# Stick-breaking attention with hi and lo parts stacked on 128 rows: two passes for scores and outputs, and suffix sums over pre-added key blocks

## What is computed

```python
h = xn @ w_in                      # [u | q | k | v | gate_a | gate_b]
z = einsum('bqhd,bkhd->bhqk', q, k) * (SB_HEAD_DIM ** -0.5)      # 8 heads of 64
causal = k_pos[None, :] < q_pos[:, None]
log_not = where(causal, log_sigmoid(-z), 0.0)
suffix = cumsum(log_not, axis=3, reverse=True) - log_not
a = where(causal, exp(log_sigmoid(z) + suffix), 0.0)
o = einsum('bhqk,bkhd->bqhd', a, v)
merged = gate_a * (y_pool @ w_pool_up) + gate_b * (o @ w_sb_up)
x = x + merged @ w_out             # then MLP, per-layer embedding, final norm
```

## Time and profile before

| | us |
|---|---|
| median of 3 runs (range) | 812.07 (811.01 to 812.73) |
| the profiled execution's own time | 810.67 |
| its span, first to last instruction | 808.9 |
| TensorE busy in the span | 790.2 |
| VectorE busy | 472.6 |
| ScalarE busy | 372.5 |
| GpSimd busy | 98.7 |

### The profile page before, as it was taken

The page is one execution under the profiler, slowest core; times in us unless marked ns, Lnnn a source line. Parts: engine busy times, 40 slices in busy tenths (PEclk is TensorE's granted clock), DMA queues, the critical chain, the costliest instruction groups (busy, mean ns, idle before and its releaser), DMA issues.

```text
span 808.9 us, 14398 instructions
## 1 busy us (share of the span) xinstructions
PE 790.2 (98%) x6130; PEld 778.7 (96%) x6130; DVE 472.6 (58%) x553; ACT 372.5 (46%) x426; POOL 98.7 (12%) x167
## 2 busy tenths in 40 slices
PE   8999999999999999999999999999999999999994
PEld 8999999999999989999999999999999999999993
DVE  6664444354356536687774257533773367677976
ACT  7444434433485343465652146422552146556543
POOL 1040140051060000010001100010001100100001
PEclk9999999999999999999999999999999999999998
DMA  6333131121221303967564865667574865825502
GB/s 231 119 119 106 66 110 61 66 92 54 91 76 44 106 27 120 294 167 176 168 201 131 196 190 178 171 172 183 167 200 121 204 193 168 211 70 141 147 1 111
DMA packets 32954, 110.19 MB, mean 136 GB/s; under 512 B 4480, under 2 KB 4480, under 8 KB 32896
## 3 DMA queue, kind: packets, MB, share of 16 engines
q1 hardware_dynamic: 24624, 84.72, 31.8%
q0 software_dynamic: 6016, 21.04, 14.5%
q10 hardware_dynamic: 2256, 3.60, 1.3%
HBM read 94.33 MB, written 4.52 MB: 122 GB/s over the span
## 4 chain that ended last, share of the span: by engine, by line
PE 90%; DVE 5%; ACT 2%; issue 1%; DMA 1%; SPq 0%; DVEq 0%
PE psum L1278 23%; PE psum L1023 19%; PE psum L1029 19%; PE psum L1026 19%; PE psum L1076 3%; PE psum L1004 2%; PE psum L1006 2%; PE psum L1005 2%; DMA raw<-w_tiles 1%; DVE work L1398 1%; DVE w_lo L1374 1%; PE psum L1356 1%; DVE xt L1818 0%; DVE b_lo L1730 0%; DVE a_lo L1594 0%
## 5 line engine op out<-in xcount | busy, mean ns | idle before, releaser
L670 ACT ACTIVATE w_hi<-raw_more 128x1024 fp32r<-128x1024 f32 x84 | 88.7, 1056 | 134.9 <-PE psum L1029 102.3
L1023 PE MATMUL psum<-b_hi,w_hi 128*128 128x272 f32 x688 | 142.3, 288 | 0.0
L1029 PE MATMUL psum<-b_hi,w_lo 128*128 128x272 f32 x688 | 142.1, 288 | 0.0
L1026 PE MATMUL psum<-b_lo,w_hi 128*128 128x272 f32 x688 | 141.9, 288 | 0.0
L1023 PE MATMUL psum<-a_hi,w_hi 128*128 128x272 f32 x576 | 121.4, 292 | 2.2 <-DVE a_lo L1388 1.9
L1382 DVE TENSOR_TENSOR w_lo<-raw_more,w_hi 128x1024 fp32r<-128x1024 f32 x84 | 102.4, 1223 | 35.6 <-ACT w_hi L670 35.4
L1029 PE MATMUL psum<-a_hi,w_lo 128*128 128x272 f32 x576 | 119.1, 288 | 0.0
L1026 PE MATMUL psum<-a_lo,w_hi 128*128 128x272 f32 x576 | 118.8, 288 | 0.0
L1278 PE MATMUL psum<-u_hi,w_hi 128*128 128x272 f32 x560 | 116.0, 288 | 1.0 <-issue 0.9
L1278 PE MATMUL psum<-u_hi,w_lo 128*128 128x272 f32 x560 | 115.7, 288 | 0.0
L1278 PE MATMUL psum<-u_lo,w_hi 128*128 128x272 f32 x560 | 115.5, 287 | 0.0
(11 more groups left out here) (207 smaller groups left out, 1006.4 us busy)
## 6 DMA issues: line engine op xcount, KB each, us to landing
raw_more<-w_tiles SPq DMA_DIRECT2D x84, 512.0 KB, 4.4
raw<-w_tiles SPq DMA_DIRECT2D x67, 512.0 KB, 3.5
raw_more<-w_tiles POOLq DMA_DIRECT2D x16, 512.0 KB, 7.0
raw_more<-raw_more POOLq DMA_DIRECT2D x14, 512.0 KB, 8.1
xt<-x_t SPq DMA_DIRECT2D x8, 272.0 KB, 5.0
y_t<-xt SPq DMA_DIRECT2D x8, 272.0 KB, 2.5
raw<-w_tiles POOLq DMA_DIRECT2D x4, 512.0 KB, 7.2
raw_more<-raw POOLq DMA_DIRECT2D x3, 512.0 KB, 5.6
```

Source lines behind the costliest of these rows:

```text
L670: act.activation(w_hi[:, t % W_RING, :, :].rearrange("p k c -> p (k c)"), src, ACT.Copy)\
L1023: pe.matmul(base[:, h, :], w_hi[:, s, wk, :], at(hi, k, h * HALF, (h + 1) * HALF), start=(opens and q == 0), stop=False, skip_group_check= ...
L1026: pe.matmul(base[:, h, :], w_hi[:, s, wk, :], at(lo, k, h * HALF, (h + 1) * HALF), start=False, stop=False, skip_group_check=True)
L1029: mm = pe.matmul(base[:, h, :], w_lo[:, s, wk, :], at(hi, k, h * HALF, (h + 1) * HALF), start=False, stop=(closes and q == len(ks) - 1), s ...
```

## The change

Scores: q's hi part of a head is put on all 128 rows (ScalarE writes its 64 rows, VectorE copies them to the other 64), the keys' hi part on the head's rows and the lo part on the other rows of one block. One pass gives hi by hi and lo by hi together; a second streams q's lo part, with zeros on the other rows (`q_low`, zeroed by GpSimd at the start). Outputs: the stationary block of a head is its v hi columns beside its v lo columns, so that one pass gives two halves of the output rows; p hi and p lo make two passes, and `head_out` copies one half from PSUM and adds the other. Sums: a key block's own and its next block are as before (the next one for one query block alone); what comes from later blocks is first added on VectorE (`stick_later`, three additions of 128 columns), cut in hi and lo (384 columns, ScalarE and VectorE) and added in one pass each. In pairs 0 to 2, `gate(3, i)` moves ahead of `stick_lo`. The new `later` buffers lie in the space of the cached keys and values, whose two loads move from behind pair 0 to behind the last `prob`.

```diff
+        later_hi = nc.alloc_sbuf_tensor_at("later_hi", [P, 3 * P], F32R, offset=place[1])
+        later_lo = nc.alloc_sbuf_tensor_at("later_lo", [P, 3 * P], F32R, offset=place[1] + 3 * P * 4)
         ckt = at(1, "ckt", [P, PAIRS, PAST])
+        later = nc.alloc_sbuf_tensor_at("later", [P, 3 * P], F32, offset=place[1])
...
+        vst = ysb[:, :, SEQ:TOK]
...
+        v_parts = b_hi[:, VOF:VOF + 2 * QB * P].rearrange("p (b n d) -> p b n d", b=QB, d=DH)
+        V_HI, V_LO = slice(0, 4, 3), slice(1, 3)
+        q_low = (b_hi[:, QLO:QLO + SEQ], q_low1[:, :])
...
+            for hh in range(2):
+                pool.memset(q_low[hh].bitcast(F32), 0.0).then_inc(const_made, 1)
...
                 act.activation(b_hi[:, SOF:SOF + Z_COLS], work[:, :], ACT.Copy).then_inc(shi_done, 1)
+                act.wait_ge(later_done, g + 1)
+                act.activation(later_hi[:, :], later[:, :], ACT.Copy).then_inc(laterhi_done, 1)
...
-                act.activation(b_hi[:, QOF:QOF + TOK], ev[:, 0, 0:TOK], ACT.Copy).then_inc(qkhi_done, 1)
+                for hh in range(2):
+                    r = rows_of(hh)
+                    act.activation(b_hi[r, QOF + hh * SEQ:QOF + (hh + 1) * SEQ], ev[r, 0, 0:SEQ], ACT.Copy)\
+                       .then_inc(qkhi_done, 1)
...
-                act.activation(b_hi[:, KOF:KOF + TOK], ev[:, 1, 0:TOK], ACT.Copy).then_inc(qkhi_done, 1)
+                for hh in range(2):
+                    r = rows_of(hh)
+                    act.activation(b_lo[r, KOF + hh * SEQ:KOF + (hh + 1) * SEQ], ev[r, 1, 0:SEQ], ACT.Copy)\
+                       .then_inc(qkhi_done, 1)
...
-            act.dma_start(ckt[:, :, :], ck_t).then_inc(past_in, 16)
-            act.dma_start(cvn[:, :, :], cv).then_inc(past_in, 16)
...
             prob(1, PAIRS - 1)
+            act.dma_start(ckt[:, :, :], ck_t).then_inc(past_in, 16)
+            act.dma_start(cvn[:, :, :], cv).then_inc(past_in, 16)
             prob_hi(1, PAIRS - 1)
...
             def scores(hh, i):
-                r = slice(DH * hh, DH * hh + DH)
-                if hh == 0:
-                    pe.wait_ge(qklo_done, 2 * i + 2)
+                pe.wait_ge(qklo_done, 6 * i + 5 + hh)
                 for b in range(QB):
                     z = z_ps[:, Z_OFF[b]:Z_OFF[b] + Z_LEN[b]]
-                    keys = slice(KOF + P * b, KOF + P * (b + 1))
-                    qs = slice(QOF + P * b, QOF + SEQ)
-                    mm = product(z, b_hi[r, keys], b_lo[r, keys], b_hi[r, qs], b_lo[r, qs], b != 3, b != 1)
+                    keys = slice(KOF + hh * SEQ + P * b, KOF + hh * SEQ + P * (b + 1))
+                    both = slice(QOF + hh * SEQ + P * b, QOF + (hh + 1) * SEQ)
+                    pe.matmul(z, b_lo[:, keys], b_hi[:, both], start=(b != 3), stop=False, skip_group_check=True)
+                    mm = pe.matmul(z, b_lo[:, keys], q_low[hh][:, P * b:SEQ], start=False, stop=(b != 1),
+                                   skip_group_check=True)
                 mm.then_inc(z_done, 1)
...
+                sticks = [(b_hi[:, SOF:SOF + Z_COLS], later_hi), (b_lo[:, SOF:SOF + Z_COLS], later_lo)]
                 for b in range(QB):
-                    for c in range(b, QB):
-                        lhs = negtri if c == b else negone
-                        z = z_ps[:, Z_OFF[b] + P * (c - b):Z_OFF[b] + Z_LEN[b]]
-                        for part in (b_hi, b_lo):
-                            mm = pe.matmul(z, lhs[:, :], part[:, SOF + Z_OFF[c]:SOF + Z_OFF[c] + Z_LEN[c]],
-                                           start=False, stop=(c == QB - 1), skip_group_check=True)
+                    at_b = Z_OFF[b]
+                    for own, _ in sticks:
+                        mm = pe.matmul(z_ps[:, at_b:at_b + Z_LEN[b]], negtri[:, :], own[:, at_b:at_b + Z_LEN[b]],
+                                       start=False, stop=(b == QB - 1), skip_group_check=True)
+                    if b == QB - 1:
+                        continue
+                    nxt = Z_OFF[b + 1]
+                    for own, _ in sticks:
+                        mm = pe.matmul(z_ps[:, at_b + P:at_b + 2 * P], negone[:, :], own[:, nxt:nxt + P],
+                                       start=False, stop=(b == QB - 2), skip_group_check=True)
+                    if b < QB - 2:
+                        more = (slice(0, 2 * P), slice(2 * P, 3 * P))[b]
+                        for _, sums_of in sticks:
+                            mm = pe.matmul(z_ps[:, at_b + 2 * P:at_b + Z_LEN[b]], negone[:, :], sums_of[:, more],
+                                           start=False, stop=True, skip_group_check=True)
                 mm.then_inc(c_done, 1)
...
-                    vs = slice(VOF + P * b, VOF + P * (b + 1))
+                    vs = slice(VOF + P * (2 * b + hh), VOF + P * (2 * b + hh + 1))
                     ps = slice(SOF + Z_OFF[b], SOF + Z_OFF[b] + Z_LEN[b])
-                    mm = product(o_ps[:, P * b:SEQ], b_hi[:, vs], b_lo[:, vs], b_hi[:, ps], b_lo[:, ps],
-                                 b == 0, b == QB - 1)
+                    pe.matmul(o_ps[:, P * b:SEQ], b_hi[:, vs], b_hi[:, ps], start=(b == 0), stop=False,
+                              skip_group_check=True)
+                    mm = pe.matmul(o_ps[:, P * b:SEQ], b_hi[:, vs], b_lo[:, ps], start=False, stop=(b == QB - 1),
+                                   skip_group_check=True)
                 mm.then_inc(o_done, 1)
...
+            def stick_later(hh, i):
+                g = 2 * i + hh
+                one, two, three = (work[:, Z_OFF[b]:Z_OFF[b] + Z_LEN[b]] for b in (1, 2, 3))
+                dve.wait_ge(spm_done, g * QB + QB)
+                dve.tensor_tensor(later[:, 2 * P:3 * P], two[:, P:2 * P], three, ALU.add).then_inc(later_part, 1)
+                dve.tensor_tensor(later[:, 0:P], one[:, P:2 * P], two[:, 0:P], ALU.add)
+                dve.wait_ge(later_part, g + 1)
+                dve.tensor_tensor(later[:, P:2 * P], one[:, 2 * P:3 * P], later[:, 2 * P:3 * P], ALU.add)\
+                   .then_inc(later_done, 1)
             def stick_lo(hh, i):
                 dve.wait_ge(shi_done, 2 * i + hh + 1)
-                dve.tensor_tensor(b_lo[:, SOF:SOF + Z_COLS], work[:, :], b_hi[:, SOF:SOF + Z_COLS],
-                                  ALU.subtract).then_inc(slo_done, 1)
+                dve.tensor_tensor(b_lo[:, SOF:SOF + Z_COLS], work[:, :], b_hi[:, SOF:SOF + Z_COLS], ALU.subtract)
+                dve.wait_ge(laterhi_done, 2 * i + hh + 1)
+                dve.tensor_tensor(later_lo[:, :], later[:, :], later_hi[:, :], ALU.subtract).then_inc(slo_done, 1)
...
             def head_out(hh, i):
-                r = slice(DH * hh, DH * hh + DH)
+                r = rows_of(hh)
                 dve.wait_ge(o_done, 2 * i + hh + 1)
-                dve.tensor_copy(ysb[r, i, 0:SEQ], o_ps[r, :]).then_inc(y_done, 1)
+                dve.tensor_copy(ysb[r, i, 0:SEQ], o_ps[rows_of(1 - hh), :]).then_inc(y_part, 1)
+                dve.wait_ge(y_part, 2 * i + hh + 1)
+                dve.tensor_tensor(ysb[r, i, 0:SEQ], o_ps[r, :], ysb[r, i, 0:SEQ], ALU.add).then_inc(y_done, 1)
...
-                dve.wait_ge(qkhi_done, 2 * i + 1)
-                dve.tensor_tensor(b_lo[:, QOF:QOF + TOK], q, b_hi[:, QOF:QOF + TOK], ALU.subtract)\
-                   .then_inc(qklo_done, 1)
+                for hh in range(2):
+                    r, twice = rows_of(hh), slice(QOF + hh * SEQ, QOF + (hh + 1) * SEQ)
+                    dve.wait_ge(qkhi_done, 4 * i + 1 + hh)
+                    dve.tensor_copy(b_hi[rows_of(1 - hh), twice], b_hi[r, twice]).then_inc(qklo_done, 1)
+                    dve.tensor_tensor(q_low[hh][r, :], q[r, 0:SEQ], b_hi[r, twice], ALU.subtract)\
+                       .then_inc(qklo_done, 1)
                 split(AHEAD + 1, i, S1_PER)
...
-                dve.wait_ge(qkhi_done, 2 * i + 2)
-                dve.tensor_tensor(b_lo[:, KOF:KOF + TOK], k, b_hi[:, KOF:KOF + TOK], ALU.subtract)\
-                   .then_inc(qklo_done, 1)
+                for hh in range(2):
+                    r, keys = rows_of(hh), slice(KOF + hh * SEQ, KOF + (hh + 1) * SEQ)
+                    dve.wait_ge(qkhi_done, 4 * i + 3 + hh)
+                    dve.tensor_tensor(b_lo[rows_of(1 - hh), keys], k[r, 0:SEQ], b_lo[r, keys], ALU.subtract)\
+                       .then_inc(qklo_done, 1)
                 split(AHEAD + 2, i, S1_PER)
...
                     split(AHEAD + 3, i, S1_PER)
+                    stick_later(0, i)
...
+                    stick_later(1, i)
                     split(AHEAD + 7, i, S1_PER)
...
                 else:
+                    gate(3, i)
+                    stick_later(1, i)
                     stick_lo(1, i)
-                    gate(3, i)
```

34 lines of the change are left out of this document (24 added, 10 removed).

## The result

The changed kernel took 801.88 us, the median of four runs from 799.16 to 803.42, beside 812.23 for the kernel before: a ratio of 0.9871, 95% interval 0.984 to 0.9902. Six more runs in another comparison gave 800.68, ratio 0.9869 (0.9844 to 0.9893); two of the seventeen executions of the kernel before there took 963 and 3979 us, at a mean granted clock of 0.75 and 0.18, and are left out. It is faster, inside the range of 796 to 803; but 798.9 had been forecast, and 801.88 is even 0.9 us above the main case's own range. Where the other 2 to 3 us are is what the experiments are about. The profiled execution took 800.98 us around a span of 798.9, 10.0 less than the span before.

The account below looks back on a forecast made before the run. TensorE was taken to bound the kernel. Savings A + B + C of 16.0 us, less 0.2 (first scores), 1.2 (last sums) and 1.4 (last outputs), made 13.2 us off the 812.07 median: 798.9 us, range 796 to 803.

Parts of the forecast that it names:

- main case: The forecast itself, 798.9 us for the whole kernel, own range 796.5 to 801; chance 0.72.
- term A: Scores and outputs of eight heads: one pass less in each list, 0.64 us per pass, 10.2 us saved.
- Term B: Around the scores: no change of array shape with 128 rows everywhere, 0.35 us per head, 2.8 us saved.
- Term C: Sums: 20 matmuls become 18 per head, 0.37 us per head, 3.0 us saved.
- Sums and outputs of the middle pairs: Added VectorE and ScalarE work fits the slack, 6.9 us before sums and 0.5 before outputs; no cost.
- Last sums: Last head: additions and splits on VectorE all become TensorE wait, cost 1.2 us, ends 0.9 and 1.9.
- Last outputs and new values: Last head: shorter outputs gain nothing (0.64), second output step adds 0.77 before `pool_part(5)`; cost 1.4 us, ends 0.6 and 1.9.
- Cached keys and values: Loads issued with the last exp: some 6 us of room for 4.7 to landing; zero cost.
- Pair 0: First scores: v's copy 1.7 us later, TensorE waits 0.2, ends 0 and 0.8; sums: nothing, at worst 0.3.
- rival 2: Late cached loads, up to 3.4 us, or outputs 0.5 us late in eight heads, 4 us; value 803; chance 0.11.
- Rival 4: TensorE's clock falls to half from 264 us to the attention stage's end at 303; 832 us, slower; chance 0.04.
- Rivals 1 and 3: First: gaps around scores not the shape's, 801.7 us, chance 0.10. Third: feeding lists set the time, 811 to 813, 0.03.

Follow-up runs that it names:

- third_pass: Changed kernel with a third pass put back in scores and outputs, on all 128 rows; median 809.31 us.
- old_sums: Changed kernel with the suffix sums done as in the kernel before, 20 matmuls per head, no sums of later blocks; median 801.22 us.
- after_again: The changed kernel run once more, unaltered, as measure for the runs beside it; 800.68 us, six runs, ratio 0.9869 to the kernel before.
- scores64: Changed kernel with both score passes reading only the head's 64 rows, same columns and number of matmuls; 803.19 us.

## Why the prediction was right, and where its number was off

- **What bounds the kernel, and term A**: right. 0.65 us per pass against 0.64; 10.4 us against 10.2.
- **Term B**: right in mechanism, 0.31 per head against 0.35; 2.5 us.
- **Term C**: 0.34 per head against 0.37; 2.7 us. The three, each measured alone, make 3.90 of the period's 4.07; 0.17 us for two heads stay unassigned. All together 16.3 us in eight heads (4 x 4.07), 16.0 predicted.
- **Sums and outputs of the middle pairs**: nothing lost, as said; between the marks there is 2.04 per head.
- **Last sums**: 1.06 us against 1.2. **Last outputs and new values**: from the exp to the new tokens' first step the gain falls by 0.74, where 1.4 of cost less the outputs' 0.64 had been put, 0.76. Both right. The sign named for this, a wait of 0.9 before `pool_part(5)`, was not worked out from that term: 0.2 of before, 0.77 added and the 0.64 that the shorter outputs turn into waiting make 1.6. It was 1.5, and 0.9 in third_pass, where the outputs are as long as before.
- **Cached keys and values**: no wait, as said.
- **Pair 0 is the term that was mis-sized**, at two places. "1.7; v ends at 35.5 instead of 33.8. TensorE waits 0.2": the copy's start moved by 2.5 us, and 0.34 more by the start of the execution, so it ended at 36.7 and TensorE waited 1.0 us, which cost 1.20. At equal start the first mark came 0.39 later, where without the wait it would have been 0.80 earlier. The sum was 1.0 too low here, and the upper end of 0.8 for this wait was too low as well. And "0.9 us of slack, 0.6 of it used; still nothing": up to the second mark another 0.65 us went, of which old_sums gives 0.5 to the additions. They did not delay these sums: the split for them ends at 50.17, and the sums start at 50.56. The delay came by another way. In pair 0 the second and third addition took 1.23 us each instead of 0.28, while GpSimd was at work:

```profile
45.71 0.29 DVE L1514 TENSOR_TENSOR later<-work 128x128 f32<-128x128 f32 x1 [0.94 <-POOL work L636]
45.92 1.23 DVE L1515 TENSOR_TENSOR later<-work 128x128 f32<-128x128 f32 x1
47.08 1.23 DVE L1517 TENSOR_TENSOR later<-work,later 128x128 f32<-128x128 f32 x1
...
50.70 1.21 DVE L1425 TENSOR_TENSOR w_lo<-raw,w_hi 128x1024 fp32r<-128x1024 f32 x1
```

  The weight split behind them started at 50.70 (49.29 before), so the buffer that it reads came free later, the next load was issued at 52.08 (50.67 before), and ScalarE waited for it with its weight copy, which stands ahead of the cut of the attention weights for the outputs. TensorE's outputs waited 0.26 us for that:

```profile
55.59 1.06 ACT L693 ACTIVATE w_hi<-raw 128x1024 fp32r<-128x1024 f32 x1 [1.23 <-DMA raw<-w_tiles]
56.56 1.26 ACT L783 ACTIVATE b_hi<-work 128x1280 fp32r<-128x1280 f32 x1
...
59.40 0.50 PE L1139 MATMUL psum<-b_hi 128*128 128x512 f32 x1 [0.26 <-DVE b_lo L1528]
```

  The profile of old_sums, which has no additions, bears this out: there ScalarE waits 0.16 us for the same load, and TensorE's first outputs do not wait.

```profile
55.13 1.06 ACT L693 ACTIVATE w_hi<-raw 128x1024 fp32r<-128x1024 f32 x1 [0.16 <-DMA raw<-w_tiles]
```

  A wait of 0.26 with the 0.24 around it is the 0.5 of old_sums. It is the first half of rival 2, the chain before the outputs that lost its slack, in one head instead of eight, by way of a weight load that the rival did not name.

  A sign of the long additions stood in the trace of before. In the kernel before, the stick's split took 1.49 us in the second head of every pair, as in the earlier trace rows, but 2.47 to 2.54 in the first head of every pair, and each time GpSimd's addition of 128x573 began within 0.04 us of it. The row that the slack in pair 0 was worked out from is a second head's.

```profile
46.29 2.47 DVE L1461 TENSOR_TENSOR b_lo<-work,b_hi 128x1280 fp32r<-128x1280 f32 x1 [2.25 <-ACT b_hi L739]
```

- **At equal clock and start** the sum thus reads 16.3 - 1.2 (the first scores) - 0.65 - 1.06 - 1.4 = 12.0 us. The marks say 11.53 and the 0.34 of the start, 11.9. Predicted were 13.2: a miss of 1.3, 1.65 too little in pair 0 less some 0.4 by which the other terms were too careful. The span of the profile before against the shortest of the changed kernel, 808.9 and 797.2, makes 11.7, but that execution has no profile to show its start.
- **Rival 4, the clock**, was priced as a fall from 264 to 303 us, 33 us of loss. That did not come. What came is its small form, stretches of 3.4 us that cost 1.6 us each, and with it the sign that the prediction had named as proving it wrong, a clock under 1 in the stage (287.4 to 290.8). By the groups of runs at least one is in eight of the ten executions of the changed kernel and in six of the fifteen of before beside after_again (in the last comparison, on another chip, in most of before's as well, median 812.74). They are the likely rest of the distance from 798.9 to the medians of 801.88 and 800.68, 1.7 and 0.5 us once pair 0 is taken off. The prediction had no case for it: the profile of before has no such stretch, but the spread of its runs, 811.01 to 812.73, was one such step wide and went unread.
- **The range** held partly by luck. Its upper end of 803 was set by rivals 1 and 2, a gap and a lost slack in all eight heads, which did not come; what took the time to 801.88, more in pair 0 than the 0.8 and 0.3 us it allowed there, and the stretches, was in none of its terms.
- Rivals 1 and 3 are out: scores64 and third_pass.

## What to carry to other kernels

Work that fills a slack in a loop's steady state still has to be placed by hand in the first and the last turn: here 16.3 us of matmul time were saved, 4.3 were paid back there, and three moves in VectorE's order, with no work less, returned 3.1 (spans of 797.2 and 794.1 without a half-clock stretch). To place them, sum the whole queue of the feeding engine from one need to the next, in order and with the rows' own durations, rather than the added pieces less the removed ones. And where the runs of one kernel stand in groups, compare executions of the same group before you argue about a few tenths of a per cent.
